# Input projection of the second block in three passes of high and low parts, with the key matrices between its units

## The reference

```python
p = (h @ w_in).astype(f32)                       # h is 512 x 1024, w_in 1024 x 4112
qkv_a, z, ab, rq, rk, rv, rg = jnp.split(p, splits, axis=-1)
q, k, v = ...                                    # convolution of 5 taps along the tokens, silu; q and k to unit length
A = jnp.where(strict, einsum(kb, kc) * decay, 0)  # keys against keys, with the decay from ab
sol = triangular_solve(A + I, [v * beta, kb * exp(G)])
# a scan over the chunks with the state S, both ways through the tokens
o_gdn = rms_norm(o_f + o_b, g) * silu(z)
rq, rk = apply_rope(rq), apply_rope(rk) * HEAD_DIM ** -0.5
o_ret = head_group_norm(r_f + r_b, g) * silu(rg) # retention: rq, rk, rv with a fixed decay
```

## Time and profile before

| | us |
|---|---|
| median of 3 runs | 1497.89 (1494.99 to 1502.27) |
| the profiled execution | 1500.46 |
| its span | 1498.6 |
| granted clock over the span | 0.968 |

### The profile page before, as it was taken

One profiled execution on the slowest core, in us unless ns is written; L12 is line 12 of the kernel. 1 busy time (PEld: TensorE's weight loads), 2 busy tenths in 40 slices (PEclk: granted clock), 3 DMA queues, 4 the chain that ended last, 5 costly groups with the idle time before them and its releaser, 6 DMA issues.

```text
span 1498.6 us, 18669 instructions
## 1 busy us (share of the span) xinstructions
PE 1377.8 (92%) x7600; PEld 1116.9 (75%) x7600; DVE 866.7 (58%) x1355; ACT 637.2 (43%) x997; POOL 62.9 (4%) x102
## 2 busy tenths in 40 slices
PE   7999999889999999899999889999847998799997
PEld 5899979667888879778888664444747986388886
DVE  4454453357889566778887445320476652566665
ACT  4445444355667556666675421100400111345553
POOL 1000000010000010000000000000330200000000
PEclk9999999999999999999999989999788999999999
DMA  9543434455445474365455642322120000545551
GB/s 360 228 170 113 169 112 162 176 183 216 178 175 204 183 257 151 127 260 190 169 197 197 244 166 99 112 98 77 58 63 7 2 1 1 224 169 193 201 175 78
DMA packets 31522, 230.12 MB, mean 154 GB/s; under 512 B 11168, under 2 KB 14624, under 8 KB 18512
## 3 DMA queue, kind: packets, MB, share of 16 engines
q1 hardware_dynamic: 19184, 217.88, 39.7%
q10 hardware_dynamic: 11248, 7.41, 1.6%
q0 software_dynamic: 1008, 3.67, 0.6%
HBM read 225.50 MB, written 3.44 MB: 153 GB/s over the span
## 4 chain that ended last, share of the span: by engine, by line
PE 81%; DVE 11%; ACT 5%; issue 2%; DMA 1%; ACTq 1%; POOL 0%; POOLq 0%; DVEq 0%
PE ps L191 25%; PE ps L418 16%; PE ps L530 13%; PE ps L469 9%; PE ps L422 8%; PE ps L460 5%; PE ps L501 2%; DVE parts L326 2%; DVE arena L1335 1%; ACT parts L322 1%; PE ps L1792 1%; ACT arena L1005 1%; ACTq L1192 1%; DVE hparts L260 1%; DVE arena L1603 1%
## 5 line engine op out<-in xcount | busy, mean ns | idle before, releaser
L326 DVE TENSOR_TENSOR parts<-ring,parts 128x1024 fp32r<-128x1024 f32 x314 | 382.8, 1223 | 265.2 <-ACT parts L322 192.7
L322 ACT ACTIVATE parts<-ring 128x1024 fp32r<-128x1024 f32 x314 | 331.5, 1057 | 276.5 <-PE ps L422 107.9
L418 PE MATMUL ps<-hparts,parts 128*128 128x512 f32 x1120 | 399.6, 401 | 8.9 <-DVE parts L326 4.0
L422 PE MATMUL ps<-hparts,parts 128*128 128x256 f32 x1120 | 316.3, 282 | 0.0
L418 PEld LDWEIGHTS ps<-hparts,parts 128*128 128x128 f32 x1120 | 212.4, 190 | 63.1 <-issue 7.9
L530 PE MATMUL ps<-parts 128*128 128x512 f32 x1032 | 240.1, 393 | 8.6 <-DVE parts L357 7.6
L530 PEld LDWEIGHTS ps<-parts 128*128 128x128 f32 x1032 | 193.6, 189 | 53.1 <-DVE parts L357 11.8
L422 PEld LDWEIGHTS ps<-hparts,parts 128*128 128x128 f32 x1120 | 214.0, 191 | 0.0
L191 PE MATMUL ps<-arena 128*128 128x128 f32 (+3 forms) x1286 | 178.4, 299 | 35.5 <-DVE arena L1637 17.6
L191 PEld LDWEIGHTS ps<-arena 128*128 128x128 f32 (+1 forms) x1286 | 166.8, 202 | 46.8 <-DVE arena L1637 17.8
L469 PE MATMUL ps<-hparts,parts 128*128 128x256 f32 x1152 | 140.4, 284 | 0.7 <-ACT arena L969 0.7
(11 more groups left out here) (212 smaller groups left out, 1040.8 us busy)
## 6 DMA issues: line engine op xcount, KB each, us to landing
ring<-in_W SPq DMA_DIRECT2D x100, 2048.0 KB, 8.1
arena<-distance_tables SPq DMA_DIRECT2D x8, 384.0 KB, 7.5
gains<-in_gains POOLq DMA_DIRECT2D x5, 512.0 KB, 7.5
ring<-in_W SPq DMA_DIRECT2D x4, 512.0 KB, 9.1
arena<-in_gate_w ACTq DMA_DIRECT2D x1, 2048.0 KB, 10.3
matrices<-arena ACTq DMA_DIRECT2D x8, 256.0 KB, 2.5
x<-in_x SPq DMA_DIRECT2D x1, 1024.0 KB, 6.2
gates<-in_ada_gate_b POOLq DMA_DIRECT2D x2, 512.0 KB, 6.5
```

The lines of the kernel that those rows point to most:

```text
L322: return nc.scalar.activation(unit_weights(n, 0, weights), weights, ACT.Copy)
L326: return nc.vector.tensor_tensor(unit_weights(n, 1, weights), weights, unit_weights(n, 0, weights), ALU.subtract)
L418: last = nc.tensor.matmul(ps[:, b, :].rearrange("p (a b) -> p a b", a=2), w[:, 0, :], hparts[:, :, k, :], start=k == 0, stop=False)
L422: last = nc.tensor.matmul(ps[:, b, 0:S], w[:, 1, :], hparts[:, 0, k, :], start=False, stop=k == KT - 1)
```

## The change

The projection is done as three products of high and low parts, in eight chunks of four units each, in a new order: keys, retention values, values, retention keys, queries, z, retention queries, retention gate. `hall` holds the parts of context and latents; for keys and values one product covers both. Both norms are evacuated as parts. `ab` is done in the same way, transposed (16 rows of 512 tokens), and turned afterwards. The transposes, `EX`, the eight matrices, their store and the gather are written between the units; each engine's order is written out by hand. The inversion stands behind the last low part, ahead of retention, and retention begins when the gate of rg is done. The tile with the level masks (`lvl`) is loaded after the last unit. Tiles move in the SBUF arena; E, squares and blocks get other places.

```diff
-            + [("win", i, 0) for i in range(8)] + [("wo2", 1, 0)] + ...
+            + [("win", i, 0) for i in WIN_ORDER] + [("wo2", 1, 0)] + ...
+WIN_ORDER = (WIN_K, WIN_RV, WIN_V, WIN_RK, WIN_Q, WIN_Z, WIN_RQ, WIN_RG)
...
-        hparts = ctx.enter_context(nc.sbuf_tensor("hparts", [P, 2, KT, S], F32R))
+        hall = ctx.enter_context(nc.sbuf_tensor("hall", [P, 2, 2, KT, S], F32R))
+        hparts = hall[:, 1]
...
+        class SplitHeads:
...
+            def unit(self, pe, n, norm=None):
+                u = self.first + n
+                pe.wait_ge(S_("low_parts"), u + 1)
+                o = self.out(n).rearrange("p (a b) -> p a b", b=S) if self.both else self.out(n)
+                for k in range(KT):
+                    if norm and k % 2 == 0:
+                        norm.bank_done(pe, k // 2)
+                    for w_part, x_part in ((0, 1), (0, 0), (1, 0)):
+                        h = hall[:, :, x_part, k, :] if self.both else hall[:, 1, x_part, k, :]
+                        last = nc.tensor.matmul(o, parts[:, u % NPARTS, w_part, k * P:(k + 1) * P], h,
+                                                start=k == 0 and x_part == 1, stop=k == KT - 1 and w_part == 1)
...
+                last.then_inc(S_("parts_used"), 1)
...
+        class SplitTokens:
...
+                for k in (2 * n, 2 * n + 1):
+                    w0 = k % 2 * 512
+                    for t, b in zip(self.tiles, self.banks):
+                        for x_part, w_part in ((1, 0), (0, 0), (0, 1)):
+                            last = nc.tensor.matmul(ps[:, b, :], hall[:, t // TT, x_part, k, t % TT * P:(t % TT + 1) * P],
+                                                    parts[:, u % NPARTS, w_part, w0:w0 + 512], ...
...
+        w_k = SplitHeads(("win", WIN_K, 0), (0, 1, 2, 3), True)
+        w_rv = SplitTokens(("win", WIN_RV, 0), (0, 1, 2, 3), (4, 5, 6, 7))
+        w_v = SplitHeads(("win", WIN_V, 0), (4, 5, 6, 7), True)
+        w_rk = SplitTokens(("win", WIN_RK, 0), (0, 1, 2, 3), (0, 1, 2, 3))
+        w_q = SplitHeads(("win", WIN_Q, 0), (4, 5, 6, 7), False)
+        w_z = SplitTokens(("win", WIN_Z, 0), LATENT, (0, 1))
+        w_rq = SplitTokens(("win", WIN_RQ, 0), LATENT, (2, 3))
+        w_rg = SplitTokens(("win", WIN_RG, 0), LATENT, (0, 1))
...
@@ scalar @@
             n_ctx.evacuate(act, 0)
             n_lat.scalar_square(act)
+            high_parts(act, u0 + 2)
             n_lat.evacuate(act, 0)
+            high_parts(act, u0 + NPARTS)
...
+            for i in range(4):
+                high_parts(act, u0 + 4 + i)
+                conv_taps(i)
+                conv_tanh(i)
             act.wait_ge(S_("ab"), 1)
+            nc_a.activation(ab_row, ps[0:16, AB_BANK, :], ACT.Copy).then_inc(S_("ab_row"), 1)
+            high_parts(act, u0 + 8)
...
+            high_parts(act, u0 + 10)
+            w_rv.done(act)
+            for t in range(TT2):
+                nc_a.activation(rv[:, t, :, :].rearrange("p a b -> p (a b)"), ps[:, w_rv.banks[t], :], ACT.Copy).then_inc(S_("tok_scalar"), 1)
+            high_parts(act, u0 + 11)
+            for i in range(TT2):
+                lengths(NORMED[i])
+            for i in range(4, 8):
+                high_parts(act, u0 + 8 + i)
+                conv_taps(i)
+                if i == 7:
                     act.wait_ge(S_("sums"), 1)
+                    nc_a.activation(EX[...], ps[:, SUMS_BANK, 0:320], ACT.Exp).then_inc(S_("EX"), 1)
+                conv_tanh(i)
+                if i == 5:
+                    for t in range(TT2):
+                        turned("knT", t)
+            for j in range(4):
+                high_parts(act, u0 + 16 + j)
+                decay(2 * j)
+                decay(2 * j + 1)
+                if j:
+                    store_matrix(2 * j - 2)
+                    store_matrix(2 * j - 1)
+            for t in range(TT2):
+                turned("v", t)
+            for n in (6, 7):
+                store_matrix(n)
+            for i in range(8, 12):
+                high_parts(act, u0 + 12 + i)
+                conv_taps(i)
+                conv_tanh(i)
+                if i == 9:
+                    act.wait_ge(S_("matrices_out"), 16 * 2 * TT2)
+                if i >= 9:
+                    gather(2 * i - 18)
+                    gather(2 * i - 17)
+            high_parts(act, u0 + 24)
+            gather(6)
+            gather(7)
+            high_parts(act, u0 + 27)
+            w_z.done(act)
+            gate_tanh(w_z, zt)
+            for i in range(TT2, TT2 + TT):
+                lengths(NORMED[i])
+            high_parts(act, u0 + 31)
+            for t in LATENT:
+                turned("qnT", t)
...
+            high_parts(act, u0 + 32)
+            w_rg.done(act)
+            gate_tanh(w_rg, rgt)
...
@@ vector @@
             n_lat.vector_scale(dve)
             n_lat.evacuate(dve, 1)
+            low_parts(dve, u0 + NPARTS)
...
+            for i in range(4):
+                low_parts(dve, u0 + 4 + i)
+                conv(i)
+            low_parts(dve, u0 + 8)
+            decay_rates()
+            low_parts(dve, u0 + 11)
+            for t in range(TT2):
+                normalized("kn", t)
+            for i in range(4, 8):
+                low_parts(dve, u0 + 8 + i)
+                conv(i)
+            for j in range(4):
+                low_parts(dve, u0 + 16 + j)
+                matrix(2 * j)
+                matrix(2 * j + 1)
             dve.wait_ge(S_("rope_in"), 16)
+            w_rk.done(dve)
+            rotated(w_rk, 0, rk[:, 0, :, :], 0)
+            rotated(w_rk, 1, rk[:, 1, :, :], 1)
+            low_parts(dve, u0 + 20)
+            conv(8)
+            rotated(w_rk, 2, rk[:, 2, :, :], 2)
+            low_parts(dve, u0 + 21)
+            conv(9)
+            rotated(w_rk, 3, rk[:, 3, :, :], 3)
+            low_parts(dve, u0 + 22)
+            conv(10)
+            low_parts(dve, u0 + 23)
+            conv(11)
+            low_parts(dve, u0 + 27)
+            for i in range(TT):
+                gated(w_z, i, zt, TT2)
+            for t in LATENT:
+                normalized("qn", t)
+            low_parts(dve, u0 + 31)
+            w_rq.done(dve)
+            rotated(w_rq, 0, rq[:, 0, :, :], 0)
+            rotated(w_rq, 1, rq[:, 1, :, :], TT2 + TT + 1)
+            low_parts(dve, u0 + 32)
...
+            invert_blocks()
+            for d in DIRS:
+                dve.wait_ge(S_("decay"), 2 * TT2 + d + 1)
+                link(v.tensor_tensor(rET[d], rET[d], bh(cst[:, C_GE if d else C_LE, :]), ALU.mult))
+            for i in range(TT):
+                gated(w_rg, i, rgt, TT2 + TT)
             for step in range(STEPS):
-                if step == 2:
-                    invert_blocks()
...
@@ tensor @@
+            n_ctx.done(pe)
+            for m in range(H4):
+                w_k.unit(pe, m, n_lat if m == 0 else None)
...
+                for w_part, x_part in ((0, 1), (0, 0), (1, 0)):
+                    last = nc.tensor.matmul(ps[0:16, AB_BANK, :]..., wab_parts[:, w_part, k, :], hall[:, :, x_part, k, :], ...
+            last.then_inc(S_("ab"), 1)
+            w_rv.unit(pe, 0)
...
+            for n in range(1, 4):
+                w_rv.unit(pe, n)
...
+            for t in range(TT2):
+                turn("kn", t)
+            for m in range(H4):
+                pe.wait_ge(S_("tok_scalar"), m + 1)
+                w_v.unit(pe, m)
+                if m == 1:
+                    for t in range(TT2):
+                        trans_done(pe, "kn", t)
+                        turn("knT", t)
+            trans_done(pe, "knT", 3)
...
+            last.then_inc(S_("sums"), 1)
+            pe.wait_ge(S_("EX"), 1)
+            for n in range(4):
+                w_rk.unit(pe, n)
+                difference(2 * n)
+                difference(2 * n + 1)
+                key_products(n)
...
+            for m in range(H4):
+                trans_done(pe, "v", m)
+                w_q.unit(pe, m)
+            pe.wait_ge(S_("tok_vector"), 2)
+            for n in range(4):
+                w_z.unit(pe, n)
...
+            pe.wait_ge(S_("tok_vector"), 4)
+            for n in range(4):
+                w_rq.unit(pe, n)
...
+                decay_transposed(d, 6 + d)
+            pe.wait_ge(S_("tok_vector"), TT2 + TT)
+            for n in range(4):
+                w_rg.unit(pe, n)
...
+            pe.wait_ge(S_("tok_vector"), TT2 + 3 * TT)
             for step in range(STEPS):
```

593 lines of the change are left out of this document (289 added, 304 removed).

## The result

The changed kernel takes 1474.03 us (median of 4 runs, 1470.07 to 1477.19) beside 1498.66 for the kernel before (1494.99 to 1502.27): ratio 0.9834, 95% interval 0.98 to 0.9869. In a second series it took 1476.75 (7 runs) beside 1495.46: 0.9873, 0.9849 to 0.9897. Forecast were 1471 us and 0.91 for faster by over 0.5%. By these medians the change is worth 24.6 us (about 20 to 30 by the interval) and 18.7 (15 to 23); forecast were 26.8.

The account below looks back on a forecast made before the run. TensorE, busy 92%, was taken as the bound, with 175.1 us of projection. Products gain 36.8 and the old middle 11.7; start, clock, waits and pre-retention give back 9, 3, 20, 11; retention loses 21.0: 1471 us, range 1455 to 1488.

Parts of the forecast that it names:

- The sum: Whole block: the delta rule starts at 1111.4 in place of 1138.2, minus 26.8 us.
- Price of the products: Projection on TensorE: 0.227 us per 512-column product, 0.122 per 256; 138.3 us of work against 175.1.
- The start: Ahead of the first key product: high and low parts of both norms delay it 9.0 us, plus 1.5 for the clock.
- EX: After the values: TensorE waits 5 us for ScalarE's exponential of the decay sums, plus 1.5 for the clock.
- z: In the z units: VectorE's work and ScalarE's gather issues stall TensorE 12 us, in gaps of 3 to 4.
- rival B: From z through rq and the first rg unit the clock stays low: 1485 us; chance 0.14 together with D.
- Before retention: After rg's turns: TensorE idles about 10 us for VectorE's inversion, masks and gates; retention starts at 1088.
- Retention: From retention's start to the delta rule, without the inversion: 6.1 + 17.3 = 23.4 us in place of 44.4.
- The check "the other way": Splits the 26.8 us gain: 21.0 from the inversion leaving retention, 5.8 from retention's earlier start, which gains 36.8 on products.
- A: Projection to retention: engines overlap, TensorE alone bounds the units, retention starts 20 us earlier: 1451 us; chance 0.18.
- C: Whole middle from EX on at 1.2 GHz: slower than before, 1529 us, or 1574 with the values; chance 0.06.
- D: Tail: the projection gains but something in ScalarE's queue costs 15 us: 1486 us; chance 0.14 together with B.

Follow-up runs that it names:

- e2: Changed kernel with VectorE making the first key unit's low part between the scaling of the latents and their evacuation, instead of behind the evacuation; 1471.6 us.
- e3: Changed kernel with ScalarE's exponential of the decay sums ahead of the third value head's tanh, instead of behind the fourth's tap; 1467.8 us.
- e4: Changed kernel with the gather's issues between a query head's first tap and its tanh on ScalarE, instead of behind the tanh; 1472.3 us.
- e6: Changed kernel with the block inversion cut into rows placed from z to the first retention state updates, leaving out the last FFN's gate bias; 1468.4 us.
- u1: Changed kernel with the block inversion back at step 2 of the retention, where it stood before the change; 1479.2 us.
- u3: Changed kernel with one float32 product of the high parts in place of three high and low products, in all eight projection parts; 1495.2 us.
- c3: One float32 product in place of three, against a 1449.2 us kernel joining four edits (early low part, earlier exponential, moved gather issues, inversion in rows); 1475.5 us.
- u4: Changed kernel with the third pass (low weights by high inputs) left out of all eight projection parts; 1452.8 us.
- e5: Changed kernel with TensorE's wait for the last retention gate moved from ahead of its first product to ahead of step 2; 1473.3 us.

## Why the prediction was right

**The sum.** The delta rule was to start at 1111.4, minus 26.8; it started at 1111.34, and M fell by 27.0. That this agrees to a tenth is partly luck: retention starts 3 us early and takes 3 us more. The medians gained less than forecast, 24.6 and 18.7 us; the second lies below by more than its interval, and what the other executions lose against the profiled ones was not found.

**Price of the products**: right. 5.74 us for 24, 11.17 for 48, 11.75 for 96 of 256 columns, the modelled end included; moving sides of two stretches ran at this pace.

**The start**: mechanism right (e2 removes it), 6.6 us instead of 9.0 between the latents' transposes and the first product. All of it came 2.3 us earlier than forecast. Two things went against each other here. The context's evacuation began at 868.83 and not at 872.5, 3.7 early; 3.05 of that lie upstream (the context's transposes begin at 867.05, before at 870.10), which nothing here explains. And from the start of the last scaling to the end of the evacuations it took 10.2 us, not the 8.9 of the last FFN. The clock there cost 3.1 (24.91 against 96 at 0.227), not 1.5.

**EX**: 4.79 us forecast as 5, the clock 1.6 to 1.9 as 1.5; e3 shows that its place was the cause. The size is partly luck. The terms that the prediction names (951.7, three cycles of 6.1, four copies at 0.5, a high part) add up to 973.1, or 974.2 with a tap (0.67) and the exponential itself (0.43), and not to 975.7; that would be a stall of 3 to 4. The trace has something that it left out: the first value head's cycle took 8.2 us on ScalarE (950.60 to 958.79), since VectorE first had to bring the keys to unit length and waited for Pool in between.

**z**: forecast a stall of 12 in gaps of 3 to 4. Measured 8.0 of waits in three unequal gaps, and about 4 of lower clock (5.35 and 4.40 us for two units, 3.0 for the others). I had put it all down to waits; e4 shows ScalarE's issues behind more than half of them. Of rival B half is right: the clock does fall again behind a gap, but not at every one (the third unit and all of rq ran at full clock). The rule of the Trainium skill ("TensorE: Matmul & The Clock Gate", section "HAM oscillation — how this bites in real kernels"), by which bursts parted by waits start anew at half clock, is borne out for the two of z's units behind waits of 4.09 and 3.13 us, not for the one behind 0.81, and for no longer than the unit itself; in e3 a unit behind a wait of 3.14 ran at full clock (3.04).

**Before retention**: TensorE idle 10.30, forecast about 10 to 11; VectorE's chain ended 3 us earlier than forecast (1084.84 against 1088): its last low part ended at 1066.2 and not 1068, and the 1.5 for handoffs was not needed, while the inversion took 15.1 instead of 14.1. That 1.0 lies in two of its products beside Pool's decayed keys, 1.25 and 0.80 us against 0.49 and 0.55 before (first row: before; the others: changed):

```profile
1111.90 0.49 DVE L1603 TENSOR_TENSOR arena<-arena 128x81 f32<-128x81 f32 x2
```

```profile
1072.09 1.25 DVE L1737 TENSOR_TENSOR row<-arena,row 128x81 f32<-128x81 f32 x2
```

```profile
1072.19 2.05 POOL L932 TENSOR_TENSOR arena<-arena 128x512 f32<-128x512 f32 x2 [19.57 <-PE ps L544]
```

**Retention**: 26.4 us against 23.4, the term that was mis-sized. I had added the old pieces on both sides of the inversion (6.1 and 17.3). But while the inversion ran there, TensorE and Pool had worked ahead for step 2. With it gone, that work shows: VectorE waits 2.19, 1.02, 0.71, 1.99 and 1.01, the first while TensorE runs at half clock. In e6, with three rows of the inversion put back between the updates, retention takes 26.8 us, hardly more than the 26.4, so the waits did have room for them.

```profile
1087.03 0.69 DVE L1720 COPY arena<-ps 128x512 f32<-128x512 f32 x1 [2.19 <-PE ps L197]
...
1095.54 2.16 DVE L1723 SCALAR_TENSOR_TENSOR arena<-arena,ps 128x128 f32<-128x128 f32 x8 [1.99 <-PE ps L197]
```

**The check "the other way"** is the step that fails as a cause. It put 21.0 us to the inversion leaving retention and 5.8 to retention's earlier start. As bookkeeping it adds up; put back by itself, the inversion costs 3 to 4 (u1), since TensorE's last turns end at 1074.6 and VectorE would then invert a little later in what is the same chain. Likewise "36.8 on products": they are worth 18 in this kernel (u3) and 26 to 31 where the waits are gone (c3, by medians and by M). A term of the sum is what one stretch loses, not what its edit is worth.

**Rivals.** A (1451: the engines overlap and TensorE alone bounds the units) was right about what lay there, wrong that this order reaches it: it takes four moves more to get 1449. B came in part, C and D not. Open: why all of z ran at the lower clock in u4 and not here, and why the first gather issue takes 2.8 us in some runs and 4.0 in others; neither was tried.

## What to carry to other kernels

When work is made cheaper for the engine that bounds a stage, list for each joint what the other engines must finish first, and in which queue it stands; here four joints held back 28 us, as much as the change gained. Take such waits out one by one, then together: here the gains of separate causes added up (28.1 against 28.4 us, one trace each). And ask what a part is worth by undoing it, not by subtracting stretches.

## What the runs showed of the hardware

- Pool and VectorE slow each other. A low part of 128x1024 took 1.88 to 1.94 us instead of 1.23 in the four retention-key cycles, beside two operations of Pool. Those took 3.02 us together, 2.04 in the kernel before, where no low part lay beside them (last row); the shortest took 1.04 us, the longest 2.02. VectorE's operations with one input in PSUM kept their time. In e5 the slow product of the inversion moved with Pool's operation.

```profile
1006.36 1.94 DVE L315 TENSOR_TENSOR parts<-ring,parts 128x1024 fp32r<-128x1024 f32 x1 [4.10 <-ACT parts L311]
1008.21 2.15 DVE L1627 SCALAR_TENSOR_TENSOR arena<-ps,arena 128x128 f32<-128x128 f32 x8
```

```profile
1006.17 3.02 POOL L925 TENSOR_TENSOR gains<-cst,arena 128x512 f32<-128x512 f32 x2 [5.09 <-PE ps L197]
```

```profile
1083.01 2.04 POOL L884 TENSOR_TENSOR arena<-cst,arena 128x512 f32<-128x512 f32 x2 [0.71 <-PE ps L191]
```

- The same start at the same place is not equally long: the first retention-key unit, behind an idle time of 4.8 us, took 7.1 to 8.6 us in seven traces that have it unchanged; the next unit, at full clock, took 5.74.
- ScalarE's one table load in the block (1.28 us at 926.07) stands ahead of the value heads: from there on exponential and tanh alternate without another, and the bound of 10 us was not needed.
